# A two-layer transformer block with a mixture of experts: one flat table-driven loop over the expert steps, with a quarter-form step for experts of up to 32 tokens

## What is computed

```python
def _moe_ffn(h, w_router, w_gate, w_up, w_down):
    logits = h.astype(jnp.float32) @ w_router.astype(jnp.float32)
    top_val, top_idx = lax.top_k(logits, TOP_K_EXPERTS)
    gate = jax.nn.softmax(top_val, axis=-1)
    ...
    def expert_block(args):
        xb, e = args
        return _swiglu(xb, w_gate[e], w_up[e], w_down[e])
```

## Time and profile before

| | |
|---|---|
| median of 3 runs | 1669.36 us (1668.28 to 1671.09) |
| the profiled execution's own time | 1672.14 us |
| its span, first to last instruction | 1670.4 us |
| TensorE busy | 1544.0 us, 92% |
| mean granted TensorE clock | 0.969 |
| loads, read from HBM | 482.63 MB |
| first expert product | 708.3 us into the span |
| last scatter product | 1658.0 us |

### The profile page before, as it was taken

The page is one execution under the profiler, slowest core; times in us unless marked ns, Lnnn a source line. Parts: engine busy times, 40 slices in busy tenths (PEclk is TensorE's granted clock), DMA queues, the critical chain, the costliest instruction groups (busy, mean ns, idle before and its releaser), DMA issues.

```text
span 1670.4 us, 21757 instructions
## 1 busy us (share of the span) xinstructions
PE 1544.0 (92%) x8696; PEld 852.4 (51%) x8697; DVE 418.1 (25%) x955; ACT 250.2 (15%) x560; POOL 0.2 (0%) x4
## 2 busy tenths in 40 slices
PE   5988889999989998599999999999999999999996
PEld 2777658777657774444444443443333443333332
DVE  2366525333344533600002000110000300003003
ACT  2132210000012331110101010011111111111112
POOL 0000000000000000000000000000000000000000
PEclk8999799999999998799999999999999999999998
DMA  9974525765656440068979797999999999997991
GB/s 348 380 266 164 189 101 192 273 252 202 227 193 229 172 178 16 1 264 332 407 289 407 284 408 294 408 374 405 408 407 407 407 377 407 407 408 296 367 377 78
DMA packets 168185, 484.43 MB, mean 290 GB/s; under 512 B 10024, under 2 KB 20544, under 8 KB 168000
## 3 DMA queue, kind: packets, MB, share of 16 engines
q1 hardware_dynamic: 168128, 483.70, 75.8%
HBM read 482.63 MB, written 1.05 MB: 290 GB/s over the span
## 4 chain that ended last, share of the span: by engine, by line
PE 79%; DMA 9%; DVE 5%; SPq 3%; ACT 2%; issue 2%; DVEq 0%; ACTq 0%
PE bank L1024 11%; PE bank L931 9%; PE bank L1064 8%; DMA ring<-in_w_exp_up 8%; PE bank L778 7%; PE bank L1008 6%; PE bank L1185 6%; PE bank L1020 5%; PE bank L949 4%; PE bank L912 4%; PE bank L1058 3%; PE bank L1211 3%; PE bank L772 3%; SPq L629 2%; PE bank L1280 2%
## 5 line engine op out<-in xcount | busy, mean ns | idle before, releaser
L1024 PE MATMUL bank<-ring,hT 128*64 128x448 f32 x1280 | 255.1, 546 | 32.2 <-DMA ring<-in_w_exp_up 12.7
L1024 PEld LDWEIGHTS bank<-ring,hT 128*64 128x64 f32 x1280 | 89.0, 137 | 190.7 <-issue 153.7
L931 PE MATMUL bank<-hT,ring 128*128 128x256 f32 x704 | 158.0, 385 | 1.7 <-DVE hT L1429 1.7
L778 PE MATMUL bank<-hT,ring 128*128 128x256 f32 x640 | 153.0, 396 | 3.9 <-ACT hT L1953 2.5
L1809 DVE TENSOR_TENSOR bt<-arena,bank 64x512 f32<-64x512 f32 (+2 forms) x36 | 24.3, 675 | 493.5 <-PE bank L1024 249.6
L931 PEld LDWEIGHTS bank<-hT,ring 128*128 128x128 f32 x704 | 135.2, 193 | 24.1 <-issue 3.8
L778 PEld LDWEIGHTS bank<-hT,ring 128*128 128x128 f32 x640 | 124.5, 198 | 26.0 <-DVE hT L1429 4.4
L1064 PE MATMUL bank<-ring,bt 128*32 128x256 f32 (+1 forms) x1232 | 136.8, 445 | 0.0
L1348 DVE SCALAR_TENSOR_TENSOR acc<-ring,cond,acc 128x512 f32<-128x512 f32 x140 | 105.2, 752 | 4.9
L1020 PE MATMUL bank<-ring,hT 128*128 128x448 f32 x256 | 100.7, 546 | 4.1 <-DMA ring<-in_w_exp_up 3.4
L1008 PE MATMUL bank<-ring,hT 128*32 128x448 f32 x1024 | 102.8, 542 | 0.0
(11 more groups left out here) (279 smaller groups left out, 1179.8 us busy)
## 6 DMA issues: line engine op xcount, KB each, us to landing
ring<-in_w_exp_gate SPq DMA_DIRECT2D x128, 896.0 KB, 9.2
ring<-in_w_exp_up SPq DMA_DIRECT2D x128, 896.0 KB, 13.0
ring<-in_w_exp_down SPq DMA_DIRECT2D x64, 1536.0 KB, 15.9
ring<-in_w_ada SPq DMA_DIRECT2D x24, 2048.0 KB, 9.4
ring<-in_w_in SPq DMA_DIRECT2D x10, 2048.0 KB, 12.8
ring<-in_w_exp_down SPq DMA_DIRECT2D x32, 512.0 KB, 16.3
ring<-in_w_ff_gate SPq DMA_DIRECT2D x5, 2048.0 KB, 12.4
ring<-in_w_ff_up SPq DMA_DIRECT2D x5, 2048.0 KB, 12.8
```

What stands on the lines that cost most here:

```text
L778: last = mm(o[:, 0:T], w[:, k, t * P:(t + 1) * P], hT[:, k, :], start=(k == 0), stop=(k == KC - 1))
L931: last = mm(bank[n % 2][:, a * T:(a + 1) * T], w[a][:, k, t * P:(t + 1) * P], hT[:, k, :], start=(k == 0), stop=(k == KC - 1))
L1024: last = mm(o[64 * c2:64 * c2 + 64, 64 * c2:64 * c2 + EH], xsT[:, k, t0:t0 + 64], w[:, k, c2 * EH:(c2 + 1) * EH], start=(k == 0), stop=(k ...
```

## The change

1. One flat loop of 21 **visits** replaces the nested loops on the three engines. A visit's number in `plan_i` packs the job, the stage ends seen, whether there is a small step, which large step, and which end follows; `visit` unpacks it. A visit is a small step, a large one, or both. Classes are read inside the visit (`class_at`, `large_class`).
2. Class 0 is new: at most 32 tokens (`TINY`). Its `tiny_step` does gate and up in the quarter form together, each product pair waiting for its own piece, then four transposes and the quarter form of the down product. The ranks go to other positions: expert 7 (28 tokens) moves to position 2 in stage 0, expert 1 (54) to stage 1, expert 5 (10) to stage 2. So stage 0 has eight tiny steps (experts 0 and 7), stage 1 four half-form ones, stage 2 four tiny ones.
3. The half-form small step does up as one product of 448 columns (`stream_hidden`), then `turn_hidden` and `down`, in place of the parts.
4. The first visit is job 0 alone. Its tokens are in slots 0 to 255, so the second gather, the large window, the clearing of `ys`, the copy of `yacc` and of the scatter weights move behind it, into an end of kind 3. The first scatter (after job 5) takes two tiles instead of one. Ends of stages look up a class before they copy bank 7.

```diff
@@ -233,8 +231,8 @@
 TURNS = (0, 1, 7, 2, 6, 3, 5, 4)
 
 
-STREAM_AT = (0, 1, 3, 5, 7, 2, 4, 6)
-NPOS = 16
+STREAM_AT = (0, 1, 3, 5, 7, 4, 6, 2)
+NPOS = 32
 LONE = 3
 JOBS = []
 for l_ in range(4):
@@ -245,12 +243,30 @@
         JOBS.append((2 * l_ + 1, s_))
         if l_ == 0:
             JOBS.append((small_, 2 * s_ % ES + 1))
-AHEAD_OF_LARGE = [n - 1 for n, (pos_, _) in enumerate(JOBS) if pos_ % 2]
-ENDS_SEEN = [0, 0, 1, 1] + [2] * 4 + [3] * 4 + [4] * 4
 JOBS_DONE = [12, 20, 28, 32]
+VISITS = []
+small_left, ends_, j_ = ES, 0, 0
+while j_ < len(JOBS):
+    has_, large_ = JOBS[j_][0] % 2 == 0, 0
+    visit_ = [j_, ends_, int(has_), 0, 0]
+    j_ += has_
+    small_left -= has_
+    end_ = 3 if has_ and j_ == 1 else int(has_ and ends_ == 0 and small_left == 0)
+    end_ = 2 if has_ and j_ in JOBS_DONE else end_
+    if not end_ and j_ < len(JOBS) and JOBS[j_][0] % 2:
+        visit_[3] = JOBS[j_][0] // 2 + 1
+        j_ += 1
+    if not end_ and (j_ == len(JOBS) or j_ in JOBS_DONE):
+        end_ = 2
+    visit_[4] = end_
+    ends_ += end_ in (1, 2)
+    VISITS.append(visit_)
+NV = len(VISITS)
+PLAN = [j + 64 * ends + 512 * has + 1024 * large + 8192 * end for j, ends, has, large, end in VISITS] + [len(JOBS)]
+NPLAN = len(PLAN)
+C_END = C_PLAN + NPLAN
 TX = 3 * P // 2
-SPLIT = 2 * P
-PARTS_AT = (0, 1, 3, 2, 4, 5, 6)
+SECOND_BANKS = (4, 5, 6, 1)
 
 
...
-
-        def jobs_done(eng, l):
-            return eng.value_load(plan_i[0:1, bass.ds(l + 32, 1)], min_val=12, max_val=32)
+        def large_class(eng, no):
+            return eng.value_load(route_i.rearrange("p a r -> p (a r)")[0:1, bass.ds(2 * no + 4 * NPOS - 1, 1)], min_val=0, max_val=4)
+
+        def planned(eng, u):
+            return eng.value_load(plan_i[0:1, bass.ds(u, 1)], min_val=0, max_val=32767)
+
+        def visit(eng, u):
+            v = planned(eng, u)
+            return [eng.snap(f) for f in (v & 63, (v >> 6) & 7, (v >> 9) & 1, (v >> 10) & 7, (v >> 13) & 3)]
...
 
-            def quarter(t0, ks):
+            def quarter(t0, ks, alone=None):
 
                 for k in ks:
                     for q, w in enumerate((eg, eg, eu, eu)):
+                        if alone is not None and k % 2 == 0 and q % 2 == 0:
+                            pe.wait_ge((full_g, full_u)[q // 2][k // 2], 16 * alone + 16)
                         last = mm(bank[2][32 * q:32 * q + 32, 64 * (q % 2):64 * (q % 2) + EH], xsT[:, k, t0:t0 + 32],
                                   w[:, k, (q % 2) * EH:(q % 2 + 1) * EH], start=(k == 0), stop=(k == KC - 1))
                         if k % 2 and q % 2:
                             last.then_inc(u_used if q == 3 else g_used, 1)
+                        elif alone is not None and k == KC - 2 and q % 2:
+                            last.then_inc(eu_p if q == 3 else eg_p, 3)
 
             def stream_hidden(J, n, i, a, t0, c=0):
...
+            def tiny_step(J, ends):
+
+                pe.wait_ge(xsS_v, ends + 1)
+                pe.wait_ge(yacc_v, 4 * ends + 12)
+                for k in range(0, KC, 2):
+                    quarter(TX, range(k, k + 2), J)
+                pe.wait_ge(yzS_v, ends + 1)
...
+                h, one_ = hs[64:P, 0, :], ident[64:P, 64:P]
+                mm(bank[3][:, 0:64], h[:, 0:P], one_, start=True, stop=True)
+                for t in range(1, 4):
+                    last = nc.tensor.transpose(bank[3][:, t * 64:(t + 1) * 64], h[:, t * P:(t + 1) * P], one_)
+                last.then_inc(et_p, 4)
+                down(J, 0, 0, ALL, (0,), 7)
...
                 pe.wait_ge(yacc_v, 4 * ends + 10)
                 stream_hidden(J, 1, 0, 0, TX)
                 pe.wait_ge(yacc_v, 4 * ends + 11)
-                up_parts(J, ends)
+                stream_hidden(J, 1, 0, 1, TX)
                 pe.wait_ge(yzS_v, ends + 1)
-                turn_parts(J)
-                pe.wait_ge(et_a, 4 * J + 2)
-                small_down(J, range(0, 2))
-                small_down(J, range(3, 4))
-                pe.wait_ge(et_a, 4 * J + 4)
-                small_down(J, (2, 4, 5, 6))
+                turn_hidden(J, 1, 0, "half", bank[3])
+                down(J, 1, 0, ALL, (0,), 7)
...
@@ -1285,25 +1280,29 @@
             PE = (mybir.EngineType.PE,)
             misfit = misfits(pe)
             with pe.If(misfit == 0):
-                pe.wait_ge(xsS_v, 1)
-                turn_scatter_weights(0, bank[3])
-                with nc.Fori(0, 4, engines=PE, head_slot={PE[0]: 0}) as l:
-                    which = class_at(pe, 2 * l + 1)
-                    with pe.Fori(0, ES) as i:
-                        J = job_ahead(pe, l, i)
-                        ends = ends_seen(pe, l, i)
-                        with pe.If(l != LONE):
+                with nc.Fori(0, NV, engines=PE, head_slot={PE[0]: 0}) as u:
+                    J, ends, has, large, end = visit(pe, u)
+                    with pe.If(has != 0):
+                        tiny = class_at(pe, 2 * ends)
+                        with pe.If(tiny == 0):
+                            tiny_step(J, ends)
+                        with pe.Else():
                             small_step(J, ends)
+                    with pe.If(large != 0):
+                        which = large_class(pe, large)
                         with pe.If(which == 3):
-                            large_step(l, J + 1, ends, 3)
+                            large_step(large, J + has, ends, 3)
                         with pe.Else():
-                            large_step(l, J + 1, ends, 2)
-                        with pe.If(l == 0):
-                            small_step(J + 2, ends)
-                            with pe.If(i == 1):
-                                stream_scatter(0, (1,))
-                    stream_scatter(l + 1, (0, 1))
+                            large_step(large, J + has, ends, 2)
+                    with pe.If(end != 0):
+                        with pe.If(end == 3):
+                            gather(1, SECOND_BANKS)
+                            turn_scatter_weights(0, bank[0])
+                            pe.wait_ge(sgt_a, 1)
+                        with pe.Else():
+                            stream_scatter(ends, (0, 1))
             with pe.Else():
+                gather(1, range(4, 8))
                 with nc.Fori(0, NE, engines=PE, head_slot={PE[0]: 0}) as r:
                     pe.wait_ge(xsT_v, r + 1)
...
@@ -1656,8 +1655,8 @@
                 signal(ins, sel_v)
 
             signal(tt(pos[:, :, 0:NE], cum, chosen, ALU.mult), dv)
-            then(ts(total, sums, float(CAPS[0]), 1.0, ALU.is_gt, ALU.add))
-            for cap in CAPS[1:]:
...
+                nc.vector.memset(bank[7][:, 0:T], 0.0).then_inc(yacc_v, 4 * NE + 1 - 20)
+                nc.vector.memset(bank[7][:, T:], 0.0).then_inc(yzS_v, 1)
+                with ve.Fori(0, NV) as u:
+                    J, ends, has, large, end = visit(ve, u)
+                    with ve.If(has != 0):
+                        with ve.If(class_at(ve, 2 * ends) == 0):
...
+                    with ve.If(end != 0):
+                        with ve.If(end == 3):
+                            stream_weights(0)
+                            gathered(1)
+                            large_window(1)
+                            signal(nc.vector.memset(ys, 0.0), dv)
+                            then(nc.vector.tensor_copy(yacc, xs[:, :, :]))
+                            for i in (4, 5, 6):
+                                last = nc.vector.memset(bank[i][:, :], 0.0)
+                            last.then_inc(yzL_v, 1)
+                            ve.wait_ge(sgt_p, 1)
+                            stream_weights(1)
```

175 lines of the change are left out of this document (63 added, 112 removed).

## The result

The changed kernel takes 1678.15 us (median of 5 runs, 1677.3 to 1680.77), the kernel before on the same chip 1670.68 (5 runs). The ratio is 1.0049, with a 95% interval from 1.0034 to 1.0063: **slower by 0.5%**, where 0.4% faster was forecast. The profiled execution took 1680.77 us, its span is 1678.9. TensorE's busy time fell from 1544.0 to 1482.3 us.

The account below looks back on a forecast made before the run. Loads and the large step's own work were taken to bound stage 0, with loads alone counting after the change. The sum 9.3 ahead - 2.0 (turns) - 1.4 (stage ends) = 5.9 us gave 1669.36 - 5.9 = 1663.5 us, range 1655 to 1671.

Parts of the forecast that it names:

- second and third cycle of stage 0: Stage-0 load cycles stay as they are, except that the middle one may go from 93.4 to 93.8 us.
- rival a: Whole kernel: TensorE's sum counts; twelve steps save 6.1 us each, the start 4 to 9; 1590 us; chance 2%.
- the stretch from J = 10 to J = 13: Stage 1: the load stream no longer breaks; 3.7 us earlier at J = 10 becomes 6.1 ahead at J = 15.
- A turn in stage 3: Loop turns at the four lone large steps: 0.5 us more each, 2.0 for four, bounds 0 and 2.4 each.
- the start: Job 0 to J = 1: J = 1 starts 4.1 us earlier, one jump and one clock fall counted, bounds 0.9 to 9.0.
- the jump to the gather: Between job 0 and the second gather: a jump over three forms that have never run, taken once at 3.17 us.
- what stands behind J = 1: Stage 0: J = 1 is unchanged, so the load issue at 756.74 us moves by 4.1; small steps are in no cycle.
- In stage 2: One more stream break, in J = 21 behind a small step, goes; the lead rises from 6.1 to 9.3 us.
- the 16 us: Tiny steps, forecast at 13.7 us where weights are there: over 16 us would show the prediction wrong.
- (b): Start lost: two jumps and clock falls leave 0 to 1 of 4.1 us, J = 12's jump breaks the stream; 1669; 16%.
- (c): Loop turns, stage 3 and two stage ends: as dear as a 3.17 us jump in place of 0.74; 1676 us; 10%.
- (d): Tiny steps' idleness lowers the clock for large steps; 1.7 us each, 5 us over three stage-0 cycles; 1668.5; 8%.

Follow-up runs that it names:

- start_old: Changed kernel with the second gather and what belongs to it put back ahead of job 0; 1666.97 us, ratio 0.9984 to the kernel before.
- warm: `start_old` plus six unused products in each tiny step's wait for SiLU and multiplication; 1666.34 us, ratio 0.9971 to the kernel before.
- no_tiny: Changed kernel with no expert counted as tiny, so all twelve small steps take the half form; 1707.15 us, ratio 1.022 to the kernel before.
- swap: `start_old` with the two large forms exchanged in TensorE's code, n = 2 first; 1672.42 us, ratio 1.0014 to the kernel before.
- half_old: Changed kernel with the half-form small step given its two up parts back; 1688.77 us, ratio 1.0105 to the kernel before.
- mid_warm: `gather_mid` plus the six unused products of `warm` in each tiny step; 1671.42 us, ratio 1.0009 to the kernel before.
- ends_first: Changed kernel with the block of stage ends at the loop body's head, run at the next visit's start; 1676.54 us, ratio 1.0044 to the kernel before.
- gather_mid: Changed kernel with the second gather placed between small and large step, first visit job 0, gather, J = 1; 1675.24 us, ratio 1.0022 to the kernel before.

## Why the prediction was wrong

**Held.** Job 0 starts 13.1 us after the first gather product (forecast 13.0). The second and third cycle of stage 0 stay at 92.5 to 93: J = 4 to J = 7 is 92.5, J = 7 to J = 10 93.0. TensorE's sum (rival a) counted for nothing, 62 us of busy time went without effect. In `start_old`, though not in the changed kernel, the stretch from J = 10 to J = 13 gives 2.9 us, where 2.4 was forecast, and the undivided half step takes 21.0 us, where 21.3 was taken. A turn in stage 3 costs 0.75 us more (forecast 0.5), 1.7 from J = 27 to J = 30.

**The step that failed is the start.** It was to bring J = 1 forward by 4.1 us and put it back by 4.9. By its own terms: job 0 takes 18.1 us, not 13.7, since the clock is low twice in it (granted 0.56 in the first 3.3 us of gate and up, which take 7.92 us against 6.23; 0.57 in the down product, 5.65 us against 3.27 in `warm`); the jump to the gather 4.77, not 3.17; the gather 9.53, where 6.9 and one fall of 1.7 were counted; a second stall of 1.90, where none was. That is 8.8 of the 9.0. The clock then costs 1.8 more in J = 1's product (20.00 against 18.24 in the earlier trace rows). A fall was sized about rightly at 1.7 us (1.7 to 2.4 here). What failed was to take one. The granted clock was low (0.50 to 0.63) four times: in the first 3.3 us of job 0, in its down product, in the first 4.5 us of the gather and in the first 4.6 us of J = 1.

**The second step is what stands behind J = 1.** The text costed stage 0 by its cycles and let the small steps vanish in them. That holds only while the small steps fit under the loads (in `no_tiny` one cycle takes 105.0 us) and while the next small step is there when its pieces land. With 6.31 us of stall and a cold product behind them, J = 2 releases its first piece too late: the issue behind it comes 31.6 us after the one behind J = 1 (759.19 to 790.80), before 27.0 (756.74 to 783.74). The stream breaks, +4.0 us. In `swap`, which has no stall there, the issue behind J = 2 comes 24.1 us after the one behind J = 1, and from J = 1 to J = 4 it is 93.5 us (760.31 to 853.85), as before the change, where the changed kernel has 97.7. The sum left the jump before J = 2 at what it had cost before, 3.17 us; it took 6.31.

**The third is the clock at the stages' ends.** From J = 10 to J = 13 the forecast had 2.4 us and the changed kernel has -0.5: the scatter (8.83 against 7.13 in `start_old`) and the half form's down product (7.87 against 6.23) ran at the low clock, 3.3 us. The stream breaks there, too (369 GB/s in its slice, where 407 was forecast). This part is not tied to the start: the same code, after the same idleness of some 2.1 us before the scatter, took 81.9 to 86.7 us for the stretch in nine kernels of this study without the filler, one execution each, and 80.4 to 83.6 in the four with it. What decides between the two is not shown. In stage 2 1.3 us came of 3.2 (2.7 in `warm`), and the last scatter took 8.71 us in place of 7.13. Tiny steps took 15.3 us (J = 11, 1064.72 to 1080.06) and more, not 13.7; the 3.3 us for the down product was right for the full clock alone. J = 0 (18.1) and J = 2 (18.8) are over the 16 us that the text named as a sign of being wrong.

Of the rivals, (b) named the mechanism, two jumps and clock falls at the start, but let them cost no more than the gain. (The chances as listed add up to 0.58, 0.28 and 0.14, not to the 0.62, 0.25 and 0.13 that are given.) (c) did not happen: a turn stays under its 2.3 us. (d) was placed at J = 4, 7 and 10, where nothing is lost; the falls that count lie in the start and at stage ends. The Trainium skill's rule on fetching (Runtime: NRT & Kernel Launch, section Instruction fetch mechanics) agrees in kind with the long stalls: packets of instructions begin in them (two in the 6.31 us before J = 2). The 1.90 us before J = 1 can't be put down to it, since no such packet begins there. But by that rule each later turn of so long a body would have to fetch again, and there the trace differs: from 790 to 1650 us the loop turned without a packet on q8. The Trainium skill's rule on short products between waits (TensorE: Matmul & The Clock Gate, section HAM oscillation) agrees in kind: granted clock 0.66 in the down product behind an idle chain, 1.00 with the filler.

**Still open.** The stalls do not grow in proportion to the code passed over. They took about 0.6 to 3, 4.8 to 7.8 or 10 to 11.7 us: 64 products more made 6.5 at one place and 0.1 at the other, 20 more in `half_old` 5.2 and 5.3, six more in `mid_warm` 5.5. That looks like one fetch more or less, by where a boundary between packets lies, but no run varied the place alone. Nor is shown why a fetch has begun early enough in `ends_first` and `swap` and not elsewhere, nor why `before` gets by with one packet and 3.17 us at its first jump over the n = 2 form, nor how the 4.2 us of the earlier gather divide between the kernel and that one execution.

## What to carry to other kernels

A table-driven loop whose body holds many forms is paid for at its first jumps, while later turns are cheap: lay the code out in the order of the first pass (`gather_mid` took the stalls before the second gather and J = 1 away so), put no jump over unused forms where nothing hides it, and look at the instruction queue's packets when a stall has no other reason. When an edit shortens work off the critical path, look at what becomes idle. The low clock that can follow the idle stretch taxes the next products, and those may be on the path. Before moving a start forward, follow the same stretch up to the first point that both orders share (here J = 1), since only what arrives there is a gain.

## What the runs showed of the hardware

- A first jump over code that has not run held TensorE for up to 11.7 us; from J = 5 on no turn of the changed kernel held it for more than 1.53. Packets of some 16 KB on the instruction queue q8 begin in the long stalls (two in 6.31 us, three in 11.73), and none begins from 790 to 1650 us.
- 64 never-executed products made the whole kernel some 8 us slower (1686.11 against 1678.15; ratios to before 1.0093 and 1.0049).
- One more register read of a table in SBUF cost TensorE 0.7 us on an exposed turn (2.18 against 1.49 us).
- Behind idle stretches of 2.8 us in tiny steps the granted clock was low again and again (0.66 in the down product of J = 11 in `start_old`). Behind some 2.1 us it was in one scatter (behind J = 19 in `start_old`, 8.83 us; in the changed kernel also behind J = 11) and not in another (before, behind J = 19: 7.13). Six products whose results nobody reads kept it at 1.00 in the down product, but not in the scatter behind J = 19 (8.74 us in `warm`).
